# Expert chunks read by row half, a gather in two steps, and unrolled loops in a two-layer backbone on one core

## The reference, cut to what matters

```python
h      = modulated_rmsnorm(x)                    # (384, 1024)
aff    = softmax(h @ router)                     # (384, 16)
for e in range(16):                              # each expert takes its best tokens:
    idx = top(aff[:, e])                         # 32 latent and 16 context tokens
    xe  = h[idx]                                 # gather
    hid = silu(xe @ w_gate[e]) * (xe @ w_up[e])  # 1024 -> 1024
    x[idx] += mod * aff[idx, e] * (hid @ w_down[e])   # scatter
```

## Time and profile before

| | |
|---|---|
| median of three runs | 2177.76 us (2175.89 to 2182.70) |
| the profiled execution | 2181.42 us, span of its core 2179.7 us |
| mean granted TensorE clock | 0.967 |
| PE busy | 1927.8 us (88%) |
| DVE, ACT, POOL busy | 614.7, 463.6, 37.0 us |
| DMA | 546.32 MB, mean 251 GB/s |

### The profile page before, as it was taken

The page is one execution under the profiler, slowest core; times in us unless marked ns, Lnnn a source line. Parts: engine busy times, 40 slices in busy tenths (PEclk is TensorE's granted clock), DMA queues, the critical chain, the costliest instruction groups (busy, mean ns, idle before and its releaser), DMA issues.

```text
span 2179.7 us, 25807 instructions
## 1 busy us (share of the span) xinstructions
PE 1927.8 (88%) x9350; PEld 994.4 (46%) x9350; DVE 614.7 (28%) x1618; ACT 463.6 (21%) x950; POOL 37.0 (2%) x64
## 2 busy tenths in 40 slices
PE   4998989998979898989779989899998899898885
PEld 3555556555543434333254556565555334342322
DVE  1122434534131212121212233353532222121212
ACT  2022321222131212121121223122213112121111
POOL 0000000000000000000000000000000000000000
PEclk8999999999979999999999999999999999999998
DMA  9224151212659999999952342413136799999993
GB/s 345 88 91 181 66 183 35 104 56 97 261 229 428 428 428 428 428 428 429 414 188 93 122 149 85 160 39 121 39 116 282 314 427 429 428 429 428 428 428 169
DMA packets 98779, 546.32 MB, mean 251 GB/s; under 512 B 6848, under 2 KB 8896, under 8 KB 73856
## 3 DMA queue, kind: packets, MB, share of 16 engines
q1 hardware_dynamic: 96384, 535.18, 60.4%
q0 software_dynamic: 2016, 9.11, 1.1%
q10 hardware_dynamic: 288, 0.84, 0.1%
HBM read 541.44 MB, written 3.67 MB: 250 GB/s over the span
## 4 chain that ended last, share of the span: by engine, by line
issue 44%; PE 43%; DMA 6%; DVE 3%; ACT 2%; DVEq 1%; POOL 1%; ACTq 0%; POOLq 0%; SPq 0%
PE bank_D L770 14%; PE bank_D L1134 8%; DMA ring<-ex_w_up 4%; PE bank_D L918 4%; PE bank_Y L1158 4%; PE bank_D L776 4%; DMA ring<-ada_w 2%; PE bank_Y L1111 1%; PE bank_Y L984 1%; PE bank_D L804 1%; PE bank_D L790 1%; PE bank_R L1172 1%; DVE EB L1951 1%; PE bank_R L1171 1%; PE bank_R L782 1%
## 5 line engine op out<-in xcount | busy, mean ns | idle before, releaser
L770 PE MATMUL bank_D<-HM,ring 128*128 128x384 f32 x1600 | 549.7, 502 | 16.8 <-ACT HM L1215 7.9
L770 PEld LDWEIGHTS bank_D<-HM,ring 128*128 128x128 f32 x1600 | 308.2, 196 | 234.2 <-issue 38.7
L1134 PE MATMUL bank_D<-ring,HM 128*64 128x512 f32 x1024 | 228.8, 594 | 18.9 <-DMA ring<-ex_w_up 14.5
L776 PE MATMUL bank_D<-ring,HM 128*128 128x512 f32 x384 | 169.5, 596 | 0.0
L1134 PEld LDWEIGHTS bank_D<-ring,HM 128*64 128x64 f32 x1024 | 72.1, 137 | 166.0 <-issue 140.1
L1947 DVE TENSOR_TENSOR EB<-EB,bank_D 128x512 f32<-128x512 f32 x32 | 22.0, 688 | 423.8 <-ACT EB L1441 423.8
L918 PE MATMUL bank_D<-YT,ring 128*128 128x384 f32 x384 | 126.1, 488 | 5.2 <-ACT YT L1194 5.2
L1158 PE MATMUL bank_Y<-ring,EB 128*64 128x512 f32 x512 | 115.2, 597 | 9.8 <-ACT EB L1194 9.8
L1134 PE MATMUL bank_D<-arena_a,HM 128*64 128x512 f32 x512 | 114.2, 593 | 5.3 <-DMA arena_a<-ex_w_gate 5.3
L776 PEld LDWEIGHTS bank_D<-ring,HM 128*128 128x128 f32 x384 | 71.5, 190 | 85.2 <-issue 83.6
L918 PEld LDWEIGHTS bank_D<-YT,ring 128*128 128x128 f32 x384 | 72.2, 190 | 54.8 <-issue 6.6
(11 more groups left out here) (248 smaller groups left out, 1858.0 us busy)
## 6 DMA issues: line engine op xcount, KB each, us to landing
ring<-ex_w_gate SPq DMA_DIRECT2D x32, 2048.0 KB, 23.6
ring<-ex_w_down SPq DMA_DIRECT2D x32, 2048.0 KB, 30.1
ring<-ex_w_up SPq DMA_DIRECT2D x32, 2048.0 KB, 24.0
ring<-ada_w SPq DMA_DIRECT2D x24, 2048.0 KB, 8.9
ring<-w_in SPq DMA_DIRECT2D x16, 2048.0 KB, 10.3
arena_a<-ex_w_gate SPq DMA_DIRECT2D x16, 2048.0 KB, 26.9
arena_a<-ex_w_up SPq DMA_DIRECT2D x16, 2048.0 KB, 21.4
arena_a<-ex_w_down SPq DMA_DIRECT2D x16, 2048.0 KB, 22.5
```

The lines of the kernel that those rows point to most:

```text
L770: last = mm(u.t[:, 0:N], w[:, kt, c * P:(c + 1) * P], src[:, kt, :], start=kt == 0, stop=kt == KT - 1)
L776: last = mm(u.t[:, :], HT[:, kt, tile(t)], w[:, kt, 0:CH], start=kt == 0, stop=kt == KT - 1)
L1134: last = mm(u.t[64 * c:64 * c + 64, :], XE[:, h * 4 + k, j, :], w[:, k, c * 512:(c + 1) * 512], start=h == 0 and k == 0, stop=h == 1 and k ...
```

## The change

Three things are changed. First, the chunks of an expert are loaded and read in the order gate half 0, up half 0, gate half 1, up half 1, down half 0, down half 1, with gate and up adding up in two banks side by side. Second, a group starts with gathers 0 and 2, then reads gate and up half 0 of its first expert, and does gathers 1 and 3 and `g_turn` only then. Third, the loops over layers and groups are unrolled in every engine's program, with counts as constants; the last group of a layer has no `next_rank` and no `next_pick`, and SP's first three loads of the program have no wait.

```diff
-EXPERT_CHUNKS = ["gate0", "gate1", "up0", "up1", "down0", "down1"]
+EXPERT_CHUNKS = ["gate0", "up0", "gate1", "up1", "down0", "down1"]
...
-def group_schedule():
-
-    s = [("gather", a) for a in range(4)] + [("g_turn",)]
+def group_schedule(g):
+
+    s = [("gather", 0), ("gather", 2)]
     for j in range(GE):
-        s += [("up", j, 0), ("up", j, 1), ("hid_turn", j), ("next_rank", j)]
-        s += ([("next_pick",)] if j == GE - 1 else []) + [("down", j)]
+        s += [("up", j, 0, 0), ("up", j, 1, 0)]
+        if j == 0:
+            s += [("gather", 1), ("gather", 3), ("g_turn",)]
+        s += [("up", j, 0, 1), ("up", j, 1, 1), ("hid_turn", j)]
+        if g < GROUPS - 1:
+            s += [("next_rank", j)] + ([("next_pick",)] if j == GE - 1 else [])
+        s += [("down", j)]
...
             def chunk_free(l, g, i):
 
-                if i % 2:
-                    last = use(here, chunk_step(i), 0, "group", g)
+                if first_half(i):
+                    sp.wait_ge(half_read, halves_read(l, g, i))
+                else:
+                    last = use(Place(l, g), chunk_step(i))
                     sp.wait_ge(last.filled, last.after)
-                else:
-                    sp.wait_ge(half_read, l * EXPERT_HALVES + g * (GE * 3) + (i // 2 + 2))
-
-            with sp.Fori(0, DEPTH) as l:
+
+            for l in range(DEPTH):
                 here.layer = l
                 for i in range(len(MIX_CHUNKS)):
...
+                    if i < MIX_RING and l == 0:
+                        pass
+                    elif i < MIX_RING:
+
+                        chunk_free(l - 1, GROUPS - 1, GROUP_CHUNKS - RING + SLOT_ORDER.index(i))
...
-                    j, x = step[1:]
+                    j, x, h = step[1:]
                     if j == 0 and x == 0:
-                        for semaphore, value in drains([use(here, ("gather", a)) for a in range(4)]):
+                        for semaphore, value in drains([use(here, ("gather", a)) for a in (h, 2 + h)]):
                             pe.wait_ge(semaphore, value)
...
-            with pe.Fori(0, DEPTH) as l:
-                here.layer, here.part = l, "layer"
+            for l in range(DEPTH):
+                here.layer, here.group = l, None
                 for step in STEPS:
                     mixer_step(l, step)
-                with pe.Fori(0, GROUPS) as g:
-                    here.group, here.part = g, "group"
-                    for step in GROUP_STEPS:
+                for g in range(GROUPS):
+                    here.group = g
+                    for step in GROUP_STEPS[g]:
                         group_step(l, g, step)
```

More of the change, by code:

```diff
@@ L281, in banks_of, with program @@
     return []
+def program():
+    for l in range(DEPTH):
+        yield l, None, STEPS
+        for g in range(GROUPS):
+            yield l, g, GROUP_STEPS[g]
+    yield DEPTH, None, END_STEPS
 def bank_uses():
-    uses = {b: {"layer": [], "group": [], "end": []} for b in BANKS}
+    count = {b: 0 for b in BANKS}
     where = {}
     turn = {"D": 0, "T": 0}
-    for part, steps in (("layer", STEPS), ("group", GROUP_STEPS), ("end", END_STEPS)):
+    for l, g, steps in program():
         for step in steps:
@@ L307, with __init__ @@
 class Use:
[L310 to L322, removed]
-            else:
-                n = n + g * len(uses["group"])
-        else:
-            n, i = DEPTH * per_layer, i
+    def __init__(self, hw, place, step, k=0):
+        at = (place.layer, place.group, step, k)
+        name, i = WHERE[at if at in WHERE else (place.layer, None, step, k)]
@@ L327, in __init__ @@
         self.t, self.filled, self.drained = hw.banks[name], hw.filled[name], hw.drained[name]
-        self.before, self.after = n + (i + 1), n + (i + 2)
-        self.bank, self.order = name, (part, i)
+        self.before, self.after = i + 1, i + 2
+        self.bank, self.order = name, i
 def drains(after, before=()):
     last = {}
-    for u, value, i in [(u, u.after, 1) for u in after] + [(u, u.before, 0) for u in before]:
-        place = (u.order[0] != "layer", u.order[1] + i)
-        if u.bank not in last or last[u.bank][0] < place:
-            last[u.bank] = (place, u.drained, value)
+    for u, value in [(u, u.after) for u in after] + [(u, u.before) for u in before]:
+        if u.bank not in last or last[u.bank][0] < value:
+            last[u.bank] = (value, u.drained, value)
@@ L570, in build, with use @@
         y_final = sem("y_final")
-        def use(place, step, k=0, part=None, group=None):
-            return Use(hw, place, step, k, part, group)
+        def use(place, step, k=0):
+            return Use(hw, place, step, k)
         block = ctx.enter_context(nc.Block())
@@ L1460, in _ @@
             fn(LAM[:, 0:2 * KT].rearrange("p (k v) -> p k v", v=2), CVEC[:, :, :], ACT.Sigmoid).then_inc(c_sigmoid, 1)
-            with act.Fori(0, DEPTH) as l:
-                here.layer, here.part = l, "layer"
+            for l in range(DEPTH):
+                here.layer, here.group = l, None
                 act.wait_ge(consts_in, 16)
@@ L1468, in _ @@
                         fence()
-                with act.Fori(0, GROUPS) as g:
-                    here.group, here.part = g, "group"
-                    for step in GROUP_STEPS:
+                for g in range(GROUPS):
+                    here.group = g
+                    for step in GROUP_STEPS[g]:
                         group_step(l, g, step)
@@ L1474, in _ @@
                             fence()
-            here.part = "end"
+            here.layer, here.group = DEPTH, None
             norm(DEPTH, 0, 2, None)
@@ L1969, in _ @@
             tt(CSIG[:, :, 0:2], LAM[:, 0:2 * KT].rearrange("p (k v) -> p k v", v=2), CVEC[:, :, :], ALU.mult).then_inc(c_ready, 1)
-            with dve.Fori(0, DEPTH) as l:
-                here.layer, here.part = l, "layer"
+            for l in range(DEPTH):
+                here.layer, here.group = l, None
                 for step in LATE_STEPS:
@@ L1975, in _ @@
                         fence()
-                with dve.Fori(0, GROUPS) as g:
-                    here.group, here.part = g, "group"
-                    for step in GROUP_STEPS:
+                for g in range(GROUPS):
+                    here.group = g
+                    for step in GROUP_STEPS[g]:
                         group_step(l, g, step)
```

90 lines of the change are left out of this document (43 added, 47 removed).

## The result

The changed kernel took 2182.21 us (median of 20 runs, 2177.69 to 2191.69). The kernel before took 2178.39 us in the same session (20 runs, 2174.09 to 2182.70). The ratio is 1.0020, 95% interval 1.0011 to 1.0028: 2.4 to 6.1 us slower, where 2170.1 and a gain of 7.7 had been forecast. The profiled execution after took 2182.11 us (span 2180.3), before 2181.42 (span 2179.7), so these two executions differ by 0.7 us where the medians differ by 3.8.

A forecast was written before the change was run, and what follows sets the result against it. PE was taken to bound the mixer stages, weight transfer by DMA the expert stages. Terms -1.4 - 4.2 - 0.8 - 0.3 - 1.0 = -7.7 us gave 2170.1 against the median 2177.76; range 2163 to 2178.

The forecast's parts named there:

- Start, -1.4: Program start: SP's first load no longer waits for `half_read` and comes at about 0.8, saving 1.4 us.
- The bound of 0: Program start: the limit of no gain, if ACT's and POOL's loads share the engines; the other bound was -1.5 us.
- Boundary, -4.2: Layer boundary: unrolling removes PE's 3.78 us pause after the last scatter and the adaLN read speeds up, saving 4.2 us.
- Start of the experts, -0.8 and -0.3: Expert stages' start: split gathers bring the first chunk and weight stream sooner, saving 0.8 us in the first layer, 0.3 in the second.
- The hole: First expert stage's start: DMA runs empty for 1.4 us before the third load, which goes out later.
- From there on nothing may starve ... this costs nothing.: Rest of the expert stages: loads keep enough margin, 5.0 us at worst, so the split gathers cost nothing.
- the margin rule: Between expert groups: loads come early enough, 7.6 us of margin at the tightest place, 5.0 left for the 27th load.
- The rival of starved code: Expert stages: straight code arrives anew past a full DMA and pauses PE, +14 us in all, 2191; chance 0.08.
- point from which it decides: Starved-code rival, expert stages: two code pauses of 3.78 us in a group, given 4.9 us free per group.
- Late clock: Expert stages' start: gaps between gathers delay PE's clock rise, costing 2.4 us a layer; 2174.9 in all; chance 0.26.
- End of the stage, 0: Expert stages' end: interleaved halves and the left-out ranks lie under PE's waits and ACT's copy, so nothing changes.
- Register work, -1.0: Whole kernel: register steps gone through unrolling, ten places on PE's path, saving 1.0 us; bounds 0 and -7.

The follow-up runs named there:

- e3: The kernel before with only its loop over the layers unrolled on SP, PE, ACT and DVE: 2174.2 us, ratio 0.9986.
- e2: The kernel before with layer and group loops unrolled, order kept, last group's ranks and the first loads' wait left out: 2179.1 us, ratio 1.0009.
- e11: e7 with gate and up chunks interleaved by halves, the four gathers kept together: 2172.9 us, ratio 0.9965 against the kernel before.
- e7: e3 with SP wholly unrolled and its first loads without a wait: 2175.6 us, ratio 0.9985 against the kernel before.
- e12: e7 with interleaved halves and split gathers, each back-to-back pair filling two banks: 2170.8 us, ratio 0.9964 against the kernel before.

## Why the prediction was wrong, step by step

- **Start, -1.4.** The load came 1.5 us sooner as said, the first adaLN read 0.9 (14.80 against 15.68), the first projection 0.7. The bound of 0 for "ACT's and POOL's loads share the engines" was the better one. The first read is 0.6 to 1.2 us sooner in all thirteen traces without the wait (14.64 to 15.08 against 15.68 to 15.80 in the four with it), but the first projection comes at 43.9 to 46.5 in the one sort and 44.8 to 46.7 in the other, so the 0.7 is a guess from two executions.
- **Boundary, -4.2.** The mechanism was right: the pause is gone in all sixteen traces of kernels with their layers unrolled, e3 among them. The size was -2.9 here, and anything from -1.2 to -2.9 in those traces (26.1 to 27.8 us against 29.0 in the one trace before). The load that is waited for went out earlier and took 11.1 us instead of 9.01, probably because it now meets more loads of the boundary. I had moved it with its old duration.
- **Start of the experts, -0.8 and -0.3.** Mis-sized. PE's part was right to 0.1 us. The hole was costed as if DMA ran at 428 GB/s until it was empty and from the moment of the next load on. The windows show 131 to 328 GB/s around it, and 279 to 360 around the fifth load: 3.2 us instead of 1.4. At the fifth load this makes +0.8 and +1.6 where -0.8 and -0.3 had been forecast.
- **"From there on nothing may starve ... this costs nothing."** This is the step that failed. No load was missing, the margin rule held, and DMA's share stayed at 1. But the stream went on to lose: 0.5 us in its mean position from the fifth load to the end of the stage in each layer, 1.2 and 0.9 in the last part's distance behind the mean, and 0.5 by the code's own bytes (0.20 MB more at 428 GB/s). With the 0.8 and 1.6 at the fifth load that is 3.0 and 3.5; measured at the last up chunk: 3.0 and 3.4. The first and the third of these terms, 1.0 together, are mostly the time that the code takes: 11 more packets of 1.06 us and two or three of 0.32 are some 12.5 us of one engine, 0.8 us spread over 16. So the step took the stream's margin for its price, and left out that the code of the unrolled groups comes in through the same 16 engines.
- **The rival of starved code.** It had the cause, group code that comes in anew past a full DMA, and set its price as pauses of PE, against which the slack of 4.9 us a group would count. No such pause appeared. The price is paid by the weight loads, where there is no slack, and so there was no point from which it decides. I gave it 0.08. The Trainium skill says in "Runtime: NRT & Kernel Launch", "Instruction fetch mechanics", that crossing into the next 16 KB of code is mostly hidden, and that kernels prefer full unrolling. The pause at the boundary agrees with its remark on branches, named in the prediction. In the expert stage the traces disagree: e2, with 15 packets of PE's code per stage against 4, reads its last up chunk 1.1 and 1.5 us later than e3.
- **Late clock.** Right, as something that happens in some executions: 2 of 6 stages, some 3 us each (459.1 against 456.2, 461.3 against 458.0). I had set 2.4, with the rise 9.4 us behind the first gather; it came 12.5 and 13.1 behind. It was not seen in the six stages with a second bank, which are too few to tell. One reading was off: in the second layer of the kernel before the clock rose at 1701.7, not at 1701.2 (a mean of 0.58 in the window from 1700 to 1702), so 3.1 us behind the first gather.
- **End of the stage, 0.** Leaving out the ranks was not free: their three short matmuls stand in PE's pause ahead of down half 0 and cut its idle time there from 1.9 to 1.5 us. Without them the clock fell there in 6 of 10 stages, 1.5 us each; with them in none of 24. Interleaving itself costs nothing, and e11 came out 2 per mille below e7, with intervals that touch.
- **Register work, -1.0.** Nothing that can be seen: the mixers less their half clock are 563.6 to 566.0 us in both kernels.

Put together on the median: -0.7 and -2.9, then +3.0 and +3.4 up to the last up chunk and 0.9 in each stage for the clock behind it, give +4.6; measured +3.8 (2.4 to 6.1). The terms come from one execution of each kernel, and the start and the boundary alone vary by some 2 us from trace to trace, so that the agreement is partly luck. The late clock, in a third of the stages of this form, would add some 2 to that, which the spread of the mixers covers.

## What to carry to other kernels

Unroll what removes a branch that PE waits for (here the layer loop), and leave a loop whose body isn't fetched again in each pass (the packets on the code queues show it) where DMA is the bound: every 16 KB of straight code is one more packet in the weight stream, and what counts is when the last part of a load lands, not the mean. If work is split to start a stream earlier, count the loads outstanding behind it, because a stream that runs down to one load pays twice. And put two matmul groups that stand back to back in two banks, even where a pause of 0.8 us seems free: with looped groups that line took the ratio from 1.0011 to 0.9964, of which the traces place 1.8 and 1.0 us in the two stages; the rest lies outside them, mostly where the clock fell in the one and not in the other, and why it did stays open.

## What the runs showed of the hardware that I had not expected

- A load of 2 MB is as late as the latest of its 16 parts. In a full stream a part that was delayed once, behind a packet of code, stayed behind for the rest of the stage: 1.9 to 2.1 us between first and last part in the kernel before, 4.3 to 5.3 in the changed one.
- DMA's share can read 0.89 to 0.97 at 279 to 360 GB/s. In a stream that restarts the share doesn't tell what is moved; the GB/s column does.
- A mixer of the same work took 584.4 us in e7's trace and 576.6 in e12's, and up to 3.8 us more or less in two executions of one kernel. Half of PE's busy time at half clock accounts for that: what is left is 561.5 to 566.1 us in all 34 mixers.
